# A hybrid decoder trunk on one core: squares of the layer norm added in pairs on POOL, variance matmuls moved into the middle of a weight unit

## What is computed

```python
def layer_norm(x, g, b):
    mu = mean(x); xc = x - mu
    var = mean(xc * xc)
    return xc * rsqrt(var + LN_EPS) * g + b

u = a * sigmoid(b)
u = causal depthwise convolution of 31 taps (u) + dw_b
u = silu(layer_norm(u, ln_g, ln_b))
yc = u @ w_conv_out
merged = sigmoid(gc) * yc + sigmoid(gp) * yp
x = x + merged @ w_out
```

## Time and profile before

| | |
|---|---|
| median of 3 runs | 1442.88 us (1442.6 to 1445.03) |
| the profiled execution: its own time | 1442.31 us |
| its span, first to last instruction | 1440.7 us |
| PE busy | 1406.9 us (98%) |
| DVE, ACT, POOL busy | 1171.1, 980.6, 236.6 us |
| chain that ended last, by engine | PE 89%, DVE 4%, issue 3%, ACT 2% |
| mean granted clock of PE | 0.992 |

### The profile page before, as it was taken

How to read it: one execution, slowest core, us unless ns; L and a number is a source line. 1 busy time by engine, 2 the same in 40 slices (tenths; PEclk the granted TensorE clock), 3 DMA queues, 4 the chain that set the end, 5 groups by cost and what they waited for, 6 DMA issues and landing times.

```text
span 1440.7 us, 18204 instructions
## 1 busy us (share of the span) xinstructions
PE 1406.9 (98%) x6438; PEld 1160.3 (81%) x6438; DVE 1171.1 (81%) x1057; ACT 980.6 (68%) x861; POOL 236.6 (16%) x249
## 2 busy tenths in 40 slices
PE   8999999999996999999999999999999999999996
PEld 6888888878884888888888888888888888888885
DVE  6987445458985888889798898888989989888895
ACT  7765443447764777767767787786786777768673
POOL 6840000005820010201201021020120102102010
PEclk9999999999998999999999999999999999999999
DMA  9656565555557799999999999999999999999990
GB/s 360 219 171 204 177 198 180 195 166 180 175 163 263 274 369 392 374 368 399 376 376 368 390 363 371 387 373 359 411 369 374 377 382 366 372 389 361 370 401 31
DMA packets 197407, 446.47 MB, mean 310 GB/s; under 512 B 8384, under 2 KB 19952, under 8 KB 197360
## 3 DMA queue, kind: packets, MB, share of 16 engines
q1 hardware_dynamic: 192496, 433.09, 80.4%
q0 software_dynamic: 2448, 8.91, 2.4%
q10 hardware_dynamic: 2416, 3.86, 0.8%
HBM read 438.49 MB, written 7.34 MB: 309 GB/s over the span
## 4 chain that ended last, share of the span: by engine, by line
PE 89%; DVE 4%; issue 3%; ACT 2%; DMA 1%; POOLq 0%; ACTq 0%; DVEq 0%; POOL 0%
PE bank L1399 28%; PE bank L1401 28%; PE bank L1400 28%; PE bank L1563 2%; DVE w_lo L947 2%; DVE dT_lo L1314 1%; ACT hT_hi L646 1%; PE bank L1673 1%; PE bank L1460 1%; ACT w_hi L646 0%; DMA gates<-xn_rows,next_rows 0%; DMA xn_rows<-tokP 0%; DVE bank L996 0%; PE bank L1525 0%; DMA work<-in_mix_norm_dram 0%
## 5 line engine op out<-in xcount | busy, mean ns | idle before, releaser
L947 DVE TENSOR_TENSOR w_lo<-raw,w_hi 128x2048 fp32r<-128x2048 f32 x257 | 585.1, 2290 | 136.2 <-ACT w_hi L646 136.1
L646 ACT ACTIVATE w_hi<-raw 128x2048 fp32r<-128x2048 f32 x257 | 491.1, 1916 | 202.8 <-PE bank L1401 202.4
L1399 PE MATMUL bank<-w_hi,dT_hi 128*128 128x512 f32 (+1 forms) x760 | 299.4, 394 | 4.0 <-DVE w_lo L947 3.0
L1401 PE MATMUL bank<-w_hi,dT_lo 128*128 128x512 f32 (+1 forms) x760 | 295.4, 389 | 0.0
L1400 PE MATMUL bank<-w_lo,dT_hi 128*128 128x512 f32 (+1 forms) x760 | 295.0, 388 | 0.0
L600 POOL TENSOR_TENSOR small<-small 128x1 f32<-128x1 f32 x17 | 65.0, 3823 | 808.3 <-DVE next_rows L1260 415.8
L1399 PE MATMUL bank<-w_hi,cT_hi 128*128 128x512 f32 x496 | 195.7, 395 | 0.0
L1401 PE MATMUL bank<-w_hi,cT_lo 128*128 128x512 f32 x496 | 193.2, 390 | 0.0
L1400 PE MATMUL bank<-w_lo,cT_hi 128*128 128x512 f32 x496 | 193.2, 389 | 0.0
L1399 PEld LDWEIGHTS bank<-w_hi,dT_hi 128*128 128x128 f32 x760 | 143.3, 189 | 35.8 <-issue 6.0
L1401 PEld LDWEIGHTS bank<-w_hi,dT_lo 128*128 128x128 f32 x760 | 143.2, 188 | 29.8
(11 more groups left out here) (234 smaller groups left out, 1826.4 us busy)
## 6 DMA issues: line engine op xcount, KB each, us to landing
raw<-in_moe_w_gate_dram SPq DMA_DIRECT2D x96, 1024.0 KB, 7.3
raw<-in_moe_w_up_dram SPq DMA_DIRECT2D x72, 1024.0 KB, 9.9
raw<-in_moe_w_down_dram SPq DMA_DIRECT2D x72, 1024.0 KB, 9.4
raw<-in_w_in_dram SPq DMA_DIRECT2D x20, 1024.0 KB, 6.2
mix<-in_moe_w_up_dram SPq DMA_DIRECT2D x16, 1024.0 KB, 8.5
gates<-in_moe_w_down_dram SPq DMA_DIRECT2D x16, 1024.0 KB, 11.0
gates<-in_moe_w_up_dram SPq DMA_DIRECT2D x16, 1024.0 KB, 8.8
work<-in_moe_w_down_dram SPq DMA_DIRECT2D x16, 1024.0 KB, 11.7
```

Of the source, the lines that this page charges most:

```text
L646: act.activation(w_hi[split_place(u)][:, 0:width], place[slot][:, 0:width], ACT.Copy).then_inc(hi_ready, 1)
L947: dve.tensor_tensor(w_lo[split_place(u)][:, 0:width], place[slot][:, 0:width], w_hi[split_place(u)][:, 0:width].bitcast(F32), ALU.subtract ...
L1399: nc.tensor.matmul(dst, a_hi, b_hi, start=start, stop=False)
L1401: return nc.tensor.matmul(dst, a_lo, b_hi, start=False, stop=stop)
```

## The change

Behind its sums of the convolution, and ahead of the gate scaling, POOL waits until both halves of the squares are there and adds the second pair of chunks to the first, in place (one 128x512 instruction per layer). PE's variance is then two matmuls (four passes) over the two remaining chunks. They leave `statistics` and become `variance`, called by a new hook `late` of `slab`: in the middle of unit U+13, after its 12 matmuls of block 0.

```diff
--- before.py
+++ after.py
@@ -352,6 +352,7 @@
         prod_ready, prod_added = sem("prod_ready"), sem("prod_added")
         pooled_done, dT_hi_ready, dT_ready = sem("pooled_done"), sem("dT_hi_ready"), sem("dT_ready")
         mean_done, centred, centred_sq, var_done = sem("mean_done"), sem("centred"), sem("centred_sq"), sem("var_done")
+        squares_added = sem("squares_added")
         std_ready, normed, silu_conv = sem("std_ready"), sem("normed"), sem("silu_conv")
         cT_ready = sem("cT_ready")
         yp_merged, yc_gated, merged_ready = sem("yp_merged"), sem("yc_gated"), sem("merged_ready")
@@ -584,6 +585,8 @@
                     pool.tensor_tensor(conv[:, c, :], part, tap_prod[:, (len(PRODUCTS) * l + n) % PRODS, :],
                                        ALU.add).then_inc(prod_added, 1)
 
+                pool.wait_ge(centred_sq, 2 * (l + 1))
+                pool.tensor_tensor(sq[:, 0:2 * S], sq[:, 0:2 * S], sq[:, 2 * S:4 * S], ALU.add).then_inc(squares_added, 1)
                 pool.wait_ge(gain_landed, seen.next(gain_landed, 16))
                 pool.wait_ge(gates_ready, seen.next(gates_ready, 2 * TB))
                 for h in range(2):
@@ -1400,7 +1403,7 @@
                 nc.tensor.matmul(dst, a_hi, b_lo, start=False, stop=False)
                 return nc.tensor.matmul(dst, a_lo, b_hi, start=False, stop=stop)
 
-            def slab(U, a_hi, a_lo, banks, fresh=None, amid=None, between=None):
+            def slab(U, a_hi, a_lo, banks, fresh=None, amid=None, between=None, late=None):
 
                 for j in range(2):
                     if U:
@@ -1418,6 +1421,8 @@
                                            k == 0, k == KD - 1)
                         if (j, b) == (0, 0) and amid is not None:
                             amid()
+                        if (j, b) == (1, 0) and late is not None:
+                            late()
                     last.then_inc(unit_used, 1)
                     if j == 0 and between is not None:
                         between()
@@ -1519,14 +1524,15 @@
                         last = nc.tensor.matmul(bank[M.mean][:, 0:S], mean_w[:, :], conv[:, c, :], start=c == 0, stop=c == CC - 1)
                     last.then_inc(mean_done, 1)
                     pool_windows(M.pooled)
-                    for c in range(CC):
-                        if c % 2 == 0:
-                            pe.wait_ge(centred_sq, seen.next(centred_sq))
-                        last = nc.tensor.matmul(bank[M.var][:, 0:S], mean_w[:, :], sq[:, c * S:(c + 1) * S], start=c == 0, stop=c == CC - 1)
+
+                def variance():
+                    pe.wait_ge(squares_added, l + 1)
+                    for c in range(2):
+                        last = nc.tensor.matmul(bank[M.var][:, 0:S], mean_w[:, :], sq[:, c * S:(c + 1) * S], start=c == 0, stop=c == 1)
                     last.then_inc(var_done, 1)
 
                 pe.wait_ge(gates_ready, seen.next(gates_ready, TB))
-                slab(U + 12, hT_hi, hT_lo, low, between=statistics)
+                slab(U + 12, hT_hi, hT_lo, low, between=statistics, late=variance)
 
                 pe.wait_ge(lo_ready, seen.at(lo_ready, pieces(U + 15)))
                 pe.wait_ge(dT_ready, seen.next(dT_ready, 2))
```

## The result

| | before | after |
|---|---|---|
| median (15 runs each) | 1443.08 us (1441.56 to 1445.46) | 1446.16 us (1444.7 to 1447.05) |
| the profiled execution | 1442.31 us | 1446.89 us |
| its span | 1440.7 us | 1445.3 us |

The ratio is 1.0018, with a 95% interval of 1.001 to 1.0026: 3.1 us more by the medians, 2.6 us (1.4 to 3.8) by the ratio, where 2.3 were forecast. It lies in the range, on the border of what I called no change. The agreement is partly luck: about 1.0 us comes from the place that I worked out, the rest from one that I never looked at.

What follows compares the result with a forecast made beforehand. PE, busy 98% of the span, bounds the kernel. Per layer 0.81 us won, 0.6 lost before the variance, 1.4 before the transposes: net 1.15, 2.3 in all, 1445.2 us from the median; range 1442.4 to 1446.6.

Steps and rivals of the forecast that it cites:

- PE's spared passes: At the variance, eight passes go and four come elsewhere: 0.81 us less PE work per layer, 1.6 us in both.
- The surcharge of up to 0.2: A pass behind an fp32r matmul could cost more than behind an fp32 pass: up to 0.2 us more per layer.
- The place: In unit U+13, PE reaches the variance at about 91.2 us, not 88.36, behind 12 matmuls of 2.7 to 2.9 us.
- Which of the two splits does it wait for?: POOL's addition, issued at 88.0 us, waits through both DVE splits, gets in at 90.59 and ends at 91.8.
- rival A: POOL gets in between DVE's two splits; reciprocal at 92.95, transposes 0.6 us later per layer, 1444.1 us in all; chance 0.25.
- The wait of 0.6 us in front of the variance: PE reaches the variance at 91.2 us and waits for POOL's addition until 91.8, in each layer.
- the root at 93.0: ACT starts the root behind the variance at 93.0 us, before at 90.46.
- the reciprocal at +1.8: DVE starts the reciprocal at about 93.5 us, not 91.70; the 1.8 us pass on to the merge, ending at 109.18.
- the mark below which I had called the prediction wrong: The prediction counts as wrong if DVE's merge ahead of PE's transposes ends before 108.5 us.
- the 1.4 of the forecast: PE's transposes wait 1.4 us per layer for DVE's merge, starting at 109.2 us though PE is there at about 107.8.
- rival C: PE's new wait in front of the transposes lowers its clock: 17 us more than the sum, 1462 us; chance 0.04.
- The shift stays as it is to the end.: Behind the transposes DVE and ACT wait for PE, not PE for them, so the delay carries unchanged to the end.

Runs made afterwards that it cites:

- run 4: Kernel after with neither move nor addition: two variance matmuls at the old place, over the first two of four chunks; 1444.87 us, ratio 1.001.
- run 3: Kernel after without POOL's addition: two variance matmuls in the middle of unit U+13, over the first two of four chunks; 1446.3 us, ratio 1.0022.
- run 6: Kernel after with 32 already fulfilled waits added on PE, bringing its program to the old length; 1443.81 us, ratio 1.001.
- run 5: Kernel before, unchanged, measured and profiled once more; 1443.23 us, ratio 1.0004.
- runs 1: Kernel before with all four variance matmuls moved to the middle of unit U+13, no addition on POOL; 1446.62 us, ratio 1.0025.
- 7: Kernel after with 16 already fulfilled waits (8 instructions) added on PE; 1443.8 us, ratio 1.0008.
- 9: Kernel before with fp32r squares, four one-pass variance matmuls at the old place, 32 fulfilled waits, DVE's merges ahead of its split of U+17; 1440.32 us, ratio 0.9984.

## Why the prediction was right, and where it was not

**PE's spared passes.** My sum had 0.81 us per layer, and that was right: 0.86 at the variance of run 4. In the kernel after, the transposes start 1.50 us behind the matmul ahead of them (107.97), so PE lost 1.27 to the wait, and with 0.50 of delay in all it had been spared 0.77. The surcharge of up to 0.2 is at most a tenth of a microsecond. What run 4 lacks to the 0.81 is the wait for the merge.

**The place.** Forecast and measured agree in kind: between run 4 and run 3 the reciprocal, the merge and the transposes all move by 1.10 us per layer, so the chain from variance to root to reciprocal to merge passes the delay on in full. Less the 0.62 us by which the merge was ahead of PE, that is the 0.5 of the kernel after. Since PE waits at the transposes, the spared passes do not enter this difference at all: they only make the wait longer. DVE's split of U+17 still waits 0.89 us for ACT (0.90 before), so nothing on ACT's side gave anything back, as costed.

**"Which of the two splits does it wait for?" That is the step that failed.** I let POOL starve through both, by the earlier trace rows, and gave that 0.6. The case that came true is rival A, which had a chance of 0.25 against the forecast's 0.6. POOL got in between them in both layers of every kernel that has the addition: 1.54 and 1.52 us in the rows above, at the price of 1.1 us for DVE's second split. The addition was ready 1.7 us ahead of PE, and run 3 shows that it costs nothing further at this place. The wait of 0.6 us in front of the variance, the root at 93.0 and the reciprocal at +1.8 fell with it; in their place stand +1.1 for the reciprocal and +0.5 for the transposes, where A had +1.25 and +0.6. The merge, at 109.42 less 0.92, ends at 108.5: exactly on the mark below which I had called the prediction wrong. The rule of the Trainium skill, "SBUF — State Buffer", section "SBUF: two separate sides", that the port pair is locked for the length of an instruction, agrees with this, and I had weighed it too lightly against one row. Why the one-element additions in the experts are overtaken (17 of them still take 3.8 us on average in the profile after) while this one is not was not tested; the two differ in size, in the length of the splits around them and in how long POOL had been idle.

**The waits and the clock.** PE waits at the transposes for 1.1 us by the profile and 1.27 by the starts of its matmuls, which is how the 1.4 of the forecast was counted, and the granted clock there stays full, as in the forecast and against rival C:

```profile
105.00:115.00 10.00, 8.89 (x44) 7.16 (x43) 9.76 (x14) 4.44 (x6) 0.00 (x0) 1.00 0.53 182
```

**"The shift stays as it is to the end."** It did, up to the last matmuls: +1.95 us at the second layer's transposes, +2.20 at the `onehot` transposes. But I took from it that nothing else changes, and a part of the program that the change doesn't touch cost 1.2 to 2.35 us (run 6 against the kernel after, by ratios and by medians), at least as much as the mechanism. No case of mine had it. The profiled execution's 4.6 us of span are 0.9 of start, 1.0 of layers, 0.25 between the layers and the end (0.2 of which the kernel before shows from one profile to the next, run 5), 2.8 at the end, less 0.4 behind the last matmul.

**The size.** So the forecast of 2.3 us was near the measured 3.1 for a partly wrong reason: the layers gave 1.0 in place of 2.3, and the end gave what was missing. With the end as it was, the change would be a loss of 0.8 us by the medians of run 6 and 1.4 by its ratio (1.001, interval 1.0001 to 1.0019), hardly to be told from nothing; the profiles give 1.0.

**What stays open** is why the length decides. In the four programs of the experiments and the one after that have the gap, PE's first scatter load starts 1.3 to 1.7 us behind the end of the DVE instruction that it waits for; in the other nine it is 0.12. The code behind the wait is reached by a jump out of the expert loop's last pass, and an instruction fetch that comes late for one placing of this code and in time for another would look like this. The traces go some way to bear that out, for they also hold the transfers that bring instructions, in the page of before:

```profile
q8 instruction: 27, 0.44, 0.1%
```

The last two of these, 16 KB each, fall at this place in every profile. PE's `onehot` transposes start 1.52 to 1.66 us behind the end of the first, in all 14; their idle time is the one that the profile puts down to "issue". The second starts 0.5 to 1.0 us behind those transposes. In the five profiles with the gap the first scatter matmul starts 1.34 to 1.51 us behind the end of the second (after: 1431.89 to 1433.29), much the same distance as with the first. In the other nine it starts between 0.23 us before that end and 0.27 behind it (before: end at 1429.74, start at 1429.54), so there PE did not wait for this transfer. That the gap is PE waiting for the second block of its program is therefore likely. It is not shown: the trace does not say for which engine a transfer is, and no run moved the code without changing its length. Nor do the runs tell why the clock is low for the last matmuls in some executions without the gap (runs 1, 7 and 9).

## What to carry to other kernels

A step moved later on the engine that is never idle must be followed along its chain to the next place where that engine needs the result, and the cover there must be known: here the result was 0.62 us ahead of PE, so four spared passes (0.8 us) could give 0.6 at best, and a result 1.1 us later cost 0.5 however many passes were spared. Cheaper passes at the old place, with the consumer's engine reordered so that it no longer waits, made a gain of both (1440.32 us). And when a change alters the number of instructions, look at the last microseconds and at jumps even though nothing there was edited, and measure a version of equal length before giving the whole difference to the mechanism.

## What was not expected of the hardware

Adding 32 fulfilled waits, 16 instructions, to PE's program made the kernel after faster (1446.16 to 1443.81 us, ratios 1.0018 to 1.001) and the fastest version too (1443.24 to 1440.32, ratios 1.0001 to 0.9984).

A POOL addition of 128x512 issued while DVE was in one split of two went in front of the second, which was ready long before, and delayed DVE by 1.1 us; a one-element addition issued in one split had also stood through the next two.

Four variance matmuls of 256 columns are recorded with 0.73 us in all in fp32r, one pass each, where the eight passes of the four fp32 ones took 1.97.
